# Forgetting attention: the causal mask moves from TensorE's scores to VectorE's decays, the score units run from wide to narrow, and GpSimd splits the early weight slabs in quarters

## The reference

```python
def fox_prompt(q, k, v, logf):
    cum = jnp.cumsum(logf, axis=1).transpose(0, 2, 1)
    def block(args):                       # 8 blocks of 128 queries
        i, qi, ci = args
        sc = jnp.einsum('bqhd,bkhd->bhqk', qi, k, preferred_element_type=jnp.float32) * SCALE
        sc = sc + ci[..., :, None] - cum[:, :, None, :]
        qpos = i * Q_BLOCK + jnp.arange(Q_BLOCK)
        sc = jnp.where(kpos[None, :] <= qpos[:, None], sc, -jnp.inf)
        p = jax.nn.softmax(sc, axis=-1)
        return jnp.einsum('bhqk,bkhd->bqhd', p.astype(v.dtype), v)
```

## Time and profile before

| | |
|---|---|
| median of 3 runs | 1516.49 us |
| the profiled execution, its own time | 1516.68 us |
| its span, first to last instruction | 1514.9 us |
| mean granted TensorE clock | 0.997 |
| PE, PEld busy | 1486.3 us, 1394.9 us |
| DVE, ACT, POOL busy | 1001.7, 609.0, 608.9 us |
| FoX phase | about 80 to 443 us of the span |

### The profile page before, as it was taken

The page is one execution under the profiler, slowest core; times in us unless marked ns, Lnnn a source line. Parts: engine busy times, 40 slices in busy tenths (PEclk is TensorE's granted clock), DMA queues, the critical chain, the costliest instruction groups (busy, mean ns, idle before and its releaser), DMA issues.

```text
span 1514.9 us, 25687 instructions
## 1 busy us (share of the span) xinstructions
PE 1486.3 (98%) x9803; PEld 1394.9 (92%) x9803; DVE 1001.7 (66%) x1913; ACT 609.0 (40%) x1265; POOL 608.9 (40%) x403
## 2 busy tenths in 40 slices
PE   7999999999999999999999999999999999999996
PEld 5999999999998999999888999999999998778885
DVE  6976566667665376865456987655555556478986
ACT  5143534435343256755232343333233333444463
POOL 5522222222232312244222678877777880000104
PEclk9999999999999999999999999999999999999998
DMA  6142223122133711258231122222222229623568
GB/s 204 54 107 76 76 96 85 50 76 67 33 114 118 240 52 34 71 182 280 98 102 45 42 86 85 85 68 75 85 85 85 80 64 328 202 92 111 186 189 158
DMA packets 156474, 165.40 MB, mean 109 GB/s; under 512 B 14005, under 2 KB 121913, under 8 KB 156353
## 3 DMA queue, kind: packets, MB, share of 16 engines
q1 hardware_dynamic: 124297, 113.80, 24.2%
q10 hardware_dynamic: 30232, 46.69, 9.3%
q0 software_dynamic: 1824, 3.28, 1.6%
HBM read 125.56 MB, written 39.85 MB: 109 GB/s over the span
## 4 chain that ended last, share of the span: by engine, by line
PE 88%; DVE 5%; POOL 2%; ACT 2%; DMA 2%; issue 1%; ACTq 0%; POOLq 0%; DVEq 0%; SPq 0%
PE bank L1213 19%; PE bank L1215 18%; PE bank L1214 18%; PE bank L1219 6%; PE bank L1221 6%; PE bank L1220 6%; PE bank L1248 4%; PE bank L1357 2%; PE bank L1328 1%; PE bank L1327 1%; POOL ring_l L1155 1%; PE bank L1718 1%; DMA gate<-d_gate 1%; PE bank L1720 1%; PE bank L1275 1%
## 5 line engine op out<-in xcount | busy, mean ns | idle before, releaser
L1213 PE MATMUL bank<-ht_h,ring_h 128*128 128x352 f32 x816 | 269.1, 330 | 0.9 <-DVE vqn L2425 0.5
L1215 PE MATMUL bank<-ht_h,ring_l 128*128 128x352 f32 x816 | 262.6, 322 | 0.0
L1214 PE MATMUL bank<-ht_l,ring_h 128*128 128x352 f32 x816 | 261.9, 321 | 0.0
L997 POOL TENSOR_TENSOR ring_h<-raw,att 128x1024 fp32r<-128x1024 f32 x40 | 84.7, 2116 | 378.4 <-PE bank L1215 370.1
L1213 PE MATMUL bank<-m_h,ring_h 128*128 128x264 f32 x648 | 184.2, 284 | 1.2 <-DVE m_l L3005 1.2
L1214 PE MATMUL bank<-m_l,ring_h 128*128 128x264 f32 x648 | 184.2, 284 | 0.0
L1215 PE MATMUL bank<-m_h,ring_l 128*128 128x264 f32 x648 | 183.9, 284 | 0.0
L1213 PEld LDWEIGHTS bank<-ht_h,ring_h 128*128 128x128 f32 x816 | 153.2, 188 | 4.3 <-issue 2.0
L1214 PEld LDWEIGHTS bank<-ht_l,ring_h 128*128 128x128 f32 x816 | 153.8, 189 | 0.7
L1215 PEld LDWEIGHTS bank<-ht_h,ring_l 128*128 128x128 f32 x816 | 153.3, 188 | 0.0
L1213 PE MATMUL bank<-tb_h,ring_h 128*128 128x264 f32 x456 | 129.9, 285 | 0.1
(11 more groups left out here) (388 smaller groups left out, 3829.9 us busy)
## 6 DMA issues: line engine op xcount, KB each, us to landing
raw<-in_w_up SPq DMA_DIRECT2D x44, 512.0 KB, 3.9
raw<-in_w_in SPq DMA_DIRECT2D x34, 512.0 KB, 3.9
rb<-in_w_down SPq DMA_DIRECT2D x66, 256.0 KB, 2.9
d_y<-conv SPq DMA_DIRECT2D x22, 529.0 KB, 3.3
d_gate<-gst ACTq DMA_DIRECT2D x48, 176.0 KB, 1.9
a<-d_y SPq DMA_DIRECT2D x33, 256.0 KB, 5.5
ra<-d_y SPq DMA_DIRECT2D x33, 256.0 KB, 2.9
gm<-d_gate ACTq DMA_DIRECT2D x8, 528.0 KB, 4.4
```

The lines of the kernel that those rows point to most:

```text
L997: order.link(nc.gpsimd.tensor_tensor(high, src, zero.to_broadcast(list(src.shape)), ALU.add))
L1213: nc.tensor.matmul(out, wh, xh, start=start, stop=False, skip_group_check=onto)
L1214: nc.tensor.matmul(out, wh, xl, start=False, stop=False, skip_group_check=onto)
L1215: return nc.tensor.matmul(out, wl, xh, start=False, stop=stop, skip_group_check=onto)
```

## The change

Units run from wide to narrow in each head: (3,1), (3,0), ... (0,0). The mask matmul of each unit goes, with the tiles `maskr` and `idr` and the two copies that made them. VectorE adds the mask to the 128 columns of `negc` of the unit's diagonal block, in place, one unit ahead (`mask_unit`); since a later unit of the head is narrower, it doesn't read those columns. At `FIRST_V` the first half of the dense chunk stands ahead of the scores. GpSimd's split of the slabs 3 up to the first slab of the FoX merge takes eight instructions of 256 columns in place of two of 1024.

```diff
-UNITS = [(h, b, r) for h in range(2) for b in range(4) for r in range(2)]
+UNITS = [(h, b, r) for h in range(2) for b in reversed(range(4)) for r in reversed(range(2))]
...
+            QUARTERS = [slice(256 * i, 256 * i + 256) for i in range(4)]
+
+            def quarter_split(n):
+                src, high, low = flat(raw[:, n % NRAW]), flat(ring_h[:, n % NSPL]), flat(ring_l[:, n % NSPL])
+                for q in QUARTERS:
+                    order.mark(nc.gpsimd.tensor_tensor(high[:, q], src[:, q], zero.to_broadcast([P, 256]), ALU.add))
+                order.catch_up()
+                for q in QUARTERS:
+                    ins = nc.gpsimd.tensor_tensor(low[:, q], src[:, q], high[:, q].bitcast(F32), ALU.subtract)
+                ins.then_inc(slab_split, 1)
...
-                    ring_split(n)
+                    if n < S_WF:
+                        quarter_split(n)
+                    else:
+                        ring_split(n)
...
-                    last = i == len(halves(b, r)) - 1
                     nc.tensor.matmul(out[:, 0:w], q, kh[:, h, o:o + w], start=True, stop=False)
-                    mm = nc.tensor.matmul(out[:, 0:w], q, kl[:, h, o:o + w], start=False, stop=not last)
-                    if last:
-
-                        mm = nc.tensor.matmul(out[:, w - P:w], idr[:, :], maskr[:, 0:P],
-                                              start=False, stop=True)
-                    mm.then_inc(s_full, 1)
+                    nc.tensor.matmul(out[:, 0:w], q, kl[:, h, o:o + w], start=False, stop=True).then_inc(s_full, 1)
...
+                    if g == FIRST_V:
+                        (n, c), = fillers(p, s)
+                        dense_chunk(n, c, part=range(KT // 2))
                     if s < NU:
...
-                        dense_chunk(n, c, part=range(KT // 2))
+                        if g != FIRST_V:
+                            dense_chunk(n, c, part=range(KT // 2))
...
-                if t == 8:
-                    dve.wait_ge(ident_in, 16)
-                    V.tensor_copy(maskr[:, :], cst[:, P:2 * P])
-                    V.tensor_copy(idr[:, :], ident).then_inc(misc_dve, 1)
...
+            def mask_unit(u):
+
+                h, b, r = UNITS[u]
+                block = negc[:, h, SPAN * b + P * r:SPAN * b + P * r + P]
+                order.mark(V.tensor_tensor(block, block, cst[:, P:2 * P], ALU.add))
...
             dve.wait_ge(negc_in, 32)
+            dve.wait_ge(ident_in, 16)
+            mask_unit(0)
...
+                        if s % HEAD_U == 0 and g:
+                            mask_unit(s)
+                        order.catch_up()
                         wait(dve, mx_ready, g)
...
                         ins.then_inc(mx_ready, 1)
+                        if (s + 1) % HEAD_U:
+                            mask_unit(s + 1)
```

More of the change, by code:

```diff
@@ L153, in program @@
     cst, o_cst = place("cst", [P, CONST_W])
-    maskr, _ = place("maskr", [P, P], F32R)
-    idr, _ = place("idr", [P, P], F32R)
     stat, _ = place("stat", [P, 64])
@@ L765, in program @@
     xp, xs = x_prompt[0], x_sample[0]
-    MD_SETUP, MD_ABS, MD_U, MD_CACHE, MD_CONV, MD_REL, MD_LOGF, MD_CUM, MD_ROWS = range(1, 10)
+    MD_ABS, MD_U, MD_CACHE, MD_CONV, MD_REL, MD_LOGF, MD_CUM, MD_ROWS = range(1, 9)
     MD_KEYS = MD_ROWS + 8
@@ L1347, in values @@
                     pe.wait_ge(v_ready, 2 * p + h + 1)
-                pe.wait_ge(t_free, at_unit[2 * v + 1] + len(halves(b, 1)))
+                pe.wait_ge(t_free, at_unit[2 * v + 1] + len(halves(*UNITS[2 * j + 1][1:])))
                 wait(pe, pv_free, v)
```

## The result

| | median of the runs, us | range | profiled span, us |
|---|---|---|---|
| before | 1516.6 (6 runs) | 1516.08 to 1517.32 | 1514.9 |
| after | 1526.45 (6 runs) | 1524.61 to 1528.81 | 1524.3 |

The ratio is 1.0066, with an interval of 1.0056 to 1.0076. The forecast was 1511.6, from 1509.3 to 1514.2: the sign is wrong, and the time lies even above rival 4 (1523.5).

The account below looks back on a forecast made before the run. TensorE was taken to bound the kernel. Masks -7.2, start +2.2, step 2 +0.6, old wait -1.2, steps 11 and 7 +0.8 - 0.1 gave -4.9 us: 1511.6 by the median, range 1509.3 to 1514.2.

Parts of the forecast that it names:

- rival 4: At seven head starts reductions slip and the transposes' banks are emptied 1.7 us late: +7, slower, 1523.5; chance 0.05.
- The mask matmuls: In the FoX phase, removing 64 mask matmuls at 0.11 us of TensorE each saves 7.2 us, bounds 3.8 and 7.7.
- the lower bound: For the removed mask matmuls: 64 x 0.06 = 3.8 us if something else short stands in front and the 0.05 stays.
- a sign against it: The forecast would be wrong if the first dense matmul behind the scores still takes 0.21 us.
- Rival 2: The exposed weight load stays: only 0.06 us per mask goes, 3.8 us, against 2.3 of new waits: 1515.0; chance 0.06.
- The start: First steps of the FoX phase: TensorE waits 1.6 and 0.5 us, taken as +2.2, then +0.6 in step 2.
- The mask add: VectorE's add of the mask to 128 columns: 0.25 us each, bounds 0.15 and 0.9.
- The old wait: TensorE's wait for DVE's normalisation in step 2, 1.1 us (1.2 in the starts), goes with the quarter splits: -1.2.
- Steps 11: In step 11 of pairs 1 to 3, row transposes wait 0.3 us each for a bank: +0.8, bounds 0 and 1.5.
- The order, later: Later FoX steps: +0.8 at steps 11, -0.1 at step 7; elsewhere about 16 us of mask adds on DVE stay hidden.
- Rival 3: DVE is late by 0.5 us in steps 1 to 3 of the seven later heads: +3.5, 1515.1; chance 0.06.
- the tail of the phase: End of the FoX phase: narrow units leave 2 us less for the cache load, which can spare it: cost 0.

Follow-up runs that it names:

- e2: Kernel before the change without its 64 mask matmuls and with no mask in their place (scores not causal): 1509.94 us.
- e4: Kernel before the change with only GpSimd's quarter splits added, for the slabs up to the FoX merge: 1514.07 us.
- e3: Kernel before the change with wide-to-narrow units and the half chunk ahead of the scores; mask matmuls and whole splits stay: 1527.78 us.
- e8: Changed kernel without its mask adds on VectorE (scores not causal): 1522.36 us.
- e1: Changed kernel with the step without a dense chunk in pairs 2 and 3 moved from step 2 to step 7: 1518.76 us.
- e7: Changed kernel with ACT's eight transfers of the cache's decays issued behind the last head's queries: 1520.87 us.
- e13: Changed kernel with the empty step moved from 2 to 7 and the cache decays' transfers issued behind the last head's queries: 1514.71 us.
- e11: Changed kernel with units narrow to wide and the half chunk behind the scores again; mask adds and quarters stay, scores not right: 1510.95 us.
- e6: Changed kernel with whole splits on GpSimd for every slab, no quarters: 1531.32 us.
- e5: Changed kernel with the low parts of the second head's keys one step later in pairs 1 to 3: 1521.97 us.
- e12: Changed kernel in the old unit order, computed rightly: masked block in its own buffer, each unit's last reduction split: 1512.65 us.

## Why the prediction was wrong

**The mask matmuls.** Right, if a little large: 6.6 us for 7.2. The difference is what the lower bound named: 16 of the 64 units end in a `kl` matmul of 128 columns, and behind those the 0.05 us stays (the first dense matmul still takes 0.21, which the forecast had named as a sign against it). 48 x 0.112 + 16 x 0.06 = 6.3. Rival 2, which had it stay everywhere, falls with e2. The forecast's "what is won there is kept" did not hold in full: e2's tail gave 1.1 us back. And its 1513.8, the whole with 5.2 us for the masks, is by the profiled execution; by the median, as the 1511.6 beside it, it is 1513.6.

**The start.** Right in place and size: 1.56, 0.41 and 0.46 us for 1.6, 0.5 and 0.6. The mask add is 0.28 us in the median, as its nearest row said (here with its minimum, median and maximum in ns, first and last start), and one is seen at 0.88 with its upper bound at 0.9:

```profile
L2567 DVE TENSOR_TENSOR negc<-negc,cst x64: 277/283/876, 77.0 to 430.5; 128x128 f32<-128x128 f32 x64
```

**The old wait.** Right: it is gone, and e4 shows the quarters as what takes it away. I had the quarters' other gain at nothing; they take away the waits at 66 and 70 us too, and the phase starts 1.3 us sooner after (in e4 1.2 for this reason). A slab costs GpSimd 1.3 us more, as forecast to be about 1: four times 663 and 801 ns for one instruction each of 2113 and 2487. The groups of GpSimd from 77 to 435 us, after:

```profile
L1002 POOL TENSOR_TENSOR ring_l<-raw,ring_h 128x256 fp32r<-128x256 f32 x81 | 62.4, 801 | 1.6
L999 POOL TENSOR_TENSOR ring_h<-raw,att 128x256 fp32r<-128x256 f32 x80 | 50.7, 663 | 238.7 <-PE bank L1227 238.7
```

**Steps 11.** Idle of 0.15, 0.15 and 0.51 us, together 0.8. But the forecast's 0.3 was one of starts, and in the starts the three are 0.31, 0.31 and 0.66 us, 1.3 together, since part of it is hidden under a busy matmul.

**The step that failed** is the one headed "The order, later": "Elsewhere 64 mask adds give DVE about 16 us ..., hidden as long as its step stays under TensorE's 5.6." That takes each step as holding a dense chunk. In pairs 2 and 3 `fillers` returns nothing for step 2, and between unit 0's and unit 1's transposes TensorE has there four short products with the values and 0.7 us of scores. I had worked out step 2 for pair 0 alone, where the chunk stands, and got 0.6 us; with the 3.8 of a chunk (2 x 1.92) taken away the same working would have given up to 4.4 (an estimate), and 2.82 was measured, twice. It is the order and not the load of the adds: without any add the wait is 2.30 us (e3) or 2.52 (e8). The low clock at 363 (3.4 us at half the rate) added 1.7. e1 moves the empty step and nothing else, and its phase is 5.1 us shorter.

**The second** is "the tail of the phase ... has as much to spare: 0". It was +5.3 us: 2.7 of wait and about as much at the lower clock. I had weighed the cache's load but not ACT's 4.5 us of issuing ahead of the last queries. In the new order TensorE gets there some 2 us sooner, as the forecast itself says; that alone brings 1.0 us (e3). What else it takes stands below, under the tail's wait. e7 gets back 5.3 us of it in the profile and 5.6 by the medians.

**Short waits and the adds.** Even e13, with both repairs, has a phase of 367.4 us where e2 has 361.0: 4.2 us more of idle and 2.2 of waits too short to show. That is the price of wide units at the head of each head and of the adds, of which I had 2.8 at the start and 0.8 later, less the 1.2 of the old wait. The rest is the 2.2 us that e1 and e13 have behind step 7 and the short waits.

**The rivals.** Rival 4 named the place (steps next to `kl`, DVE late, seven head starts at 1.7 us) and had the sign. But its mechanism was even lateness, and the runs show two places at 2.8 us and five heads with hardly any idle. Its "against" (wide units beside `kl` in steps 12 and 15 never waited) was true of steps that have a chunk. Rival 3 was too small for the same reason.

**What the parts leave over.** Taken one by one they give 1516.6 + 11.5 (e3) - 6.3 (e2) - 2.2 (e4) + 2.4 (adds, e11) = 1522.0, where 1526.45 was measured. Of these 4.4 us some 3.3 are the tail: its excess over before is 5.3 us after, and 2.0 in the same sum of e3, e2, e4 and e11. Another 1.0 is that the waits of step 2 are 2.82 and not 2.30.

**Which parts make the tail's wait.** The runs tell it together. The reversed order with the mask matmuls in place (e3) waits 0.81 us there, and the missing mask matmuls in the old order (e2) 0.88. Both together wait 2.67 us without the quarters (e6) and 2.68 without the adds (e8), as after, so neither the quarters nor the adds by themselves are needed for it. In every run the long wait goes with which of two instructions starts first: VectorE's low part of the last queries, or GpSimd's over 1024 columns. In e2 VectorE is ahead by 0.03 us:

```profile
440.28 1.22 DVE L2535 SCALAR_TENSOR_TENSOR qsw<-vqn,qsw 64x1024 fp32r<-64x1024 f32 x1 [0.64 <-ACT qsw L1755]
...
440.31 2.94 POOL L997 TENSOR_TENSOR ring_h<-raw,att 128x1024 fp32r<-128x1024 f32 x1 [11.81 <-PE bank L1215]
```

Here GpSimd pays (2.94 us for 1.89), and so it does in e3 and e11 (ahead by 0.11 and 0.13). In after, e1, e5, e6 and e8 VectorE is 0.66 to 0.81 us behind, and its low part takes 2.20 to 2.32 us for 1.22. The issue of the eight transfers itself took 3.8 us in before, e3, e4 and e12 and 4.5 to 4.9 in after, e1, e2, e5, e6, e8 and e11; why stays open.

## What to carry to other kernels

Before an order is turned round, list what the bounding engine has in every step, in each iteration of the outer loop, and look first at the steps whose filler table is empty: an average of 5.6 us a step hides nothing in a step of 0.7. Work that ends a chain (wide units at the end) may be what covers an issue burst of another engine; price that cover before it is moved. And where a trick needs a costly order (adding in place), a small buffer that frees the order can be worth its extra instructions: 1512.65 us against 1526.45.

## What the runs showed of the hardware

The clock did not fall after each idle of one size. After idles of 2.82 us it stayed high at 272 and fell to its lower level at 363, in the same kernel; e7 did the same with 2.72 twice, e3 fell at 277.6 and not at 368 (2.30 both), e8 at neither (2.52); e5 fell after one of two idles of only 2.18. At the tail, after 2.67 to 2.72 us, it fell in all of after, e1, e5, e6 and e8, for 3.4 us in e1 and e6 and 6.8 in the others. So a wait there costs up to about twice what it shows: 5.3 us of tail for 2.7 of wait.

VectorE's instructions take longer beside GpSimd's whole splits, and in sum by more than I had thought. Without quarters VectorE is busy for 1034 us in the same program, with them for 1005:

```profile
PE 1486.7 (97%) x9739; PEld 1392.3 (91%) x9739; DVE 1034.3 (68%) x1975; ACT 609.7 (40%) x1265; POOL 606.8 (40%) x403
```

(the page of e6_no_quarters, to be set against that of after). VectorE wins 29 us of busy time for 35 that GpSimd pays. In the old order (e4 against before) it is 13 us (1001.7 to 988.7) for 42 (608.9 to 651.1).
